# Four column blocks of x, the first weight split behind the turns, bias rows spread in DRAM, and fences given in two halves

## The chip, the cores and the metric

One core of one Trainium2 chip runs the whole program in one launch. The metric is device time in microseconds (us), the median of repeated executions; smaller is better.

## The reference

Two transformer layers are applied to 256 tokens of width 2048, all in float32. What matters here is the head of the first one and where its results go:

```python
h    = rms_norm(x, norm_mix)            # x: 256 x 2048
proj = h @ w_in                         # 2048 x 6168, cut into q, k, v, gates of three mixers
bias = rel_table[t5_bucket(distance)]   # one value per head and distance, 12 heads (layer 1), 8 heads (layer 2)
p    = exp(q @ k.T * scale + bias - max) ...
x    = x + mixed @ w_out;  x = x + cross_attention(...);  x = x + conv_ffn(...)     # layer 1
x    = x + (g_a * (nsa @ w_pa) + g_b * (deltanet @ w_pb)) @ w_o                     # layer 2
x    = x + square(relu(rms_norm(x) @ w_up)) @ w_down
```

Every dense product is one of 24 "gemms" over weights of about 500 MB in all. The two attentions with a relative bias add, for a query i and a key j, a value that depends on i - j and the head alone.

## The kernel before

**The gemms.** Weights lie in DRAM as items of 128 x 2048 float32 (1 MB; four k-tiles by 512 columns). SyncE issues one DMA for each item into one of four buffers `w_raw` (`Gemm.load`, L170); the load of item i+4 waits until VectorE has made the low part of item i. ScalarE rounds an item to `w_hi` (`make_hi`, L189), VectorE subtracts to get `w_lo` (`make_lo`, L194); both have two buffers, so the high part of item i+2 waits until TensorE is done with item i. TensorE multiplies each item three times (hi*hi, lo*hi, hi*lo; L282 to L284) for each of the two token tiles: 24 matmuls of 128x512. The left operand is `h_hi`/`h_lo`: x turned on TensorE against `ident` (L428, 32 transposes for 2048 columns), scaled by the gain and rounded on ScalarE (L441), its rest taken on VectorE (L455).

**Stages.** The program is a list of stages that TensorE, ScalarE and VectorE all walk through. After a stage each of them drains, signals, and waits for the two others (`stage_end`, L739), except where the stage is marked `unmet`: then nobody waits. Stage "start" loads nothing itself: its ScalarE part makes item 0's high part and waits for the gains and x, its VectorE part makes the low part, and all three meet. Stage "norm_mix" then turns x (`norm_to_lhs`, which calls `to_lhs`), makes item 1 on both engines and takes the root of the mean square of tile 0. Stage "win" is the first gemm: eight chunks of four items.

**The bias tables.** After the first chunk (items 0 to 3) TensorE multiplies the relative tables by a one-hot matrix (`toe_pe`, L810), VectorE adds (`toe_dve`, L816) and leaves two small tiles `tsum`: 12 and 8 partitions of 384 values. GpSimd's queue (`toe_pool`) writes each of these rows to DRAM 128 times over (`toe1`, `toe2`, laid out head, partition, value; L800), waits for both, and then goes on to the tables `tri`, `cmask` and the small weights. Much later `toeplitz` (L971) reads row p of a head's 128 copies with a start that moves by one value a partition, which gives the matrix over i - j.

**Together.** Five stages run a gemm and other work interleaved (`Together`). The work is cut into parts; after each gemm item q every engine does its share of parts (`done < (q+1) * parts // Q`), and ahead of them ScalarE and VectorE make the parts of item q+1. Between two works stands a fence (`pieces`): drain, add to the own `fenced` semaphore, wait for the two others. It stands at the head of the next work's first part. Where the next work's first part falls in the same item as the last part before it, nothing is between them; where it falls in the next item, the drain and the signal come after that item's `make_hi`/`make_lo` (or its 24 matmuls). The split of parts over items puts a gemm item between these works: small1 and turn1; small2 and turn2; turn2 and flat; unit2 and turn_qk; rates and delta0; state0 and delta1; gnorm and turn_ob (four items). After a stage's last work there is a fence too, and then the stage's own meeting.

Of the kernel before, what the change touches and what calls it, by code (L numbers as in the profile page):

```python
# [6 lines left out]
F32 = mybir.dt.float32  # L7
# [5 lines left out]
P = 128  # L13
S = 256
TT = S // P
D = 2048
KD = D // P
# [3 lines left out]
CH = 512  # L21
# [5 lines left out]
A_W, A_H, A_D = 768, 12, 64  # L27
# [11 lines left out]
N_H, N_G, N_D = 8, 2, 128  # L39
# [6 lines left out]
TOE = 384  # L46
# [25 lines left out]
def build(nc, t_in, out):  # L72

    ctx = ExitStack()
    with ctx:
# [3 lines left out]
        def sem(name):  # L79
            return ctx.enter_context(nc.semaphore(name))  # L80
# [16 lines left out]

        acc = [ctx.enter_context(nc.psum_tensor(f"acc{i}", [P, 512], F32)) for i in range(2)]
        wk = [ctx.enter_context(nc.psum_tensor(f"wk{i}", [P, 512], F32)) for i in range(6)]
        toe1 = nc.dram_tensor("toe1_scratch", (A_H, P, TOE), F32, kind="Internal").ap()  # L100
        toe2 = nc.dram_tensor("toe2_scratch", (N_H, P, TOE), F32, kind="Internal").ap()


        raw_ready = [sem(f"raw_ready{i}") for i in range(RAW)]
# [8 lines left out]
        stages = []  # L113


        class Gemm:
# [47 lines left out]
            def load(self, e):  # L164
                def body(n, first):
                    for j in range(self.ipc):
                        i = self.b + n * self.ipc + j
                        if not (first and self.b + j < RAW):
                            e.wait_ge(lo_ready, i - RAW + 1)
                        e.dma_start(w_raw[:, (self.slot(n, j)) % RAW, 0:self.cols(j)],  # L170
                                    self.w[bass.ds(n * self.ipc + j, 1), :, 0:self.cols(j)].rearrange(
                                        "a p f -> p (a f)")).then_inc(raw_ready[self.slot(n, j) % RAW], 16)
                self.chunks(e, body)
# [189 lines left out]
        class Together:  # L363
# [10 lines left out]

            def pieces(self, k, e):
                for i, w in enumerate(self.work):
                    yield from w.walk(k, e)

                    e.drain().then_inc(fenced[k], 1)
                    for other in fenced:  # L380
                        if other != k:
                            e.wait_ge(fenced[other], self.base + i + 1)

            def run(self, k, e):
                items = [(g, n, j) for g in self.gemms for n in range(g.n) for j in range(g.ipc)]
# [25 lines left out]
        turned_lo = sem("turned_lo")  # L411
        turns = [0]

        def to_lhs(src, n, hi, lo, kt0=0, gain=None):


            base = turns[0]
            turns[0] += n // 2
            W = len(wk)

            def pe(e):
                for p in range(n // 2):
                    if p >= W:
                        e.wait_ge(turned_lo, base + p - W + 1)
                    for i in (2 * p, 2 * p + 1):
                        for t in range(TT):
                            c = (i % 2) * S + t * P
                            mm = pe_.matmul(wk[p % W][:, c:c + P], src(t, i), ident[:], start=True, stop=True,  # L428
                                            is_transpose=True)
                    mm.then_inc(turned, 1)  # L430

            def act(e):
                for p in range(n // 2):
                    e.wait_ge(turned, base + p + 1)
                    b = wk[p % W]
                    if gain is None:
                        ins = act_.activation(hi[:, kt0 + 2 * p:kt0 + 2 * p + 2, :],
                                              b[:].rearrange("p (c s) -> p c s", c=2), ACT.Copy)
                    else:
                        for i in (2 * p, 2 * p + 1):  # L440
                            ins = act_.activation(hi[:, kt0 + i, :], b[:, (i % 2) * S:(i % 2 + 1) * S], ACT.Copy,  # L441
                                                  scale=gain[:, i:i + 1])
                    ins.then_inc(turned_hi, 1)

            def dve(e):
                for p in range(n // 2):
                    e.wait_ge(turned_hi, base + p + 1)
                    b = wk[p % W]
                    if gain is None:
                        k = slice(kt0 + 2 * p, kt0 + 2 * p + 2)  # L450
                        ins = dve_.tensor_tensor(lo[:, k, :], b[:].rearrange("p (c s) -> p c s", c=2),
                                                 hi[:, k, :].bitcast(F32), ALU.subtract)
                    else:
                        for i in (2 * p, 2 * p + 1):
                            ins = dve_.scalar_tensor_tensor(out=lo[:, kt0 + i, :], in0=b[:, (i % 2) * S:(i % 2 + 1) * S],  # L455
                                                            scalar=gain[:, i:i + 1], in1=hi[:, kt0 + i, :].bitcast(F32),
                                                            op0=ALU.mult, op1=ALU.subtract)
                    ins.then_inc(turned_lo, 1)
            return pe, act, dve
# [71 lines left out]
                e.wait_ge(squared, self.base + t + 1)  # L531
                return dve_.reciprocal(self.inv(t), st[:, 2 + t:3 + t])

        def norm_to_lhs(name, src, rows, hi, lo, gain, need=None):

            norm = Norm()
            norm.of(src, lambda t: rows[:, t, :])
            base = turns[0]  # L540
            tp, ta, td = to_lhs(lambda t, i: src[:, t, i * P:(i + 1) * P], KD, hi, lo, gain=gain)

            def pe(e):
                if need:
                    need(e)
                tp(e)

            def act(e):
                if need:
                    need(e)  # L550
                ta(e)
                norm.gemm.make_hi(e, 0, 1)
                norm.root(e, 0)

            def dve(e):
                td(e)
                norm.gemm.make_lo(e, 0, 1)
                norm.inverse(e, 0).then_inc(scaled, 1)
            s = Steps(name, pe, act, dve)
            s.unmet = True  # L560
            s.norm, s.lhs_from = norm, (base, 0)
            return s
# [194 lines left out]
        def got(e, name):  # L757
            if name not in landed:
                landed[name] = sem("in_" + name)
            e.wait_ge(landed[name], 16)  # L760
# [17 lines left out]

        rows0 = p1[:, :, 0:D]

        toe_mm, toe_row, toe_out, toe_dma = sem("toe_mm"), sem("toe_row"), sem("toe_out"), sem("toe_dma")
        tt1f = tt1[:].rearrange("p a b -> p (a b)")

        def toe_place(rows, slot, w):
# [6 lines left out]
        def toe_pool(e):  # L791
            for i in range(2):
                load(e, f"tw{i}", tw[i], t_in[f"onehot{i}"])
                load(e, f"trel{i}", trel[i], t_in[f"rel{i}"])
                load(e, f"tadd{i}", tadd[i], t_in[f"toe_add{i}"])
            e.wait_ge(toe_out, 2)


            for table, row, heads in ((toe1, tsum[0], A_H), (toe2, tsum[1], N_H)):
                e.dma_start(table, row.unsqueeze(1).to_broadcast([heads, P, TOE])).then_inc(toe_dma, 16)  # L800
            e.wait_ge(toe_dma, 32)
            load(e, "tri", tri[:], t_in["tri"])
            load(e, "cmask", cmask[:], t_in["cmask"])
        pool_steps.append(toe_pool)

        def toe_pe(e):
# [10 lines left out]

        def start_pe(e):
            got(e, "ident")
            got(e, "x")  # L820

        def start_dve(e):
            dve_.memset(ones[:], 1.0)
            dve_.memset(eps_c[:], EPS)
            Gemm.every[0].make_lo(e, 0, 0)
            got(e, "gains")

        def start_act(e):
            Gemm.every[0].make_hi(e, 0, 0)
            got(e, "gains")  # L830
            got(e, "x")
        stages.append(Steps("start", start_pe, start_act, start_dve))
        stages.append(norm_to_lhs("norm_mix", x, rows0, h_hi, h_lo, gains[:, 0, :]))
        mix = stages[-1]
        lhs = (h_hi, h_lo)

# [123 lines left out]
        def toeplitz(e, name, dst, table, heads, at_stage):  # L960

            landed[name] = sem("in_" + name)
            for k, sems in (at_stage.items() if isinstance(at_stage, dict) else ((k, at_stage) for k in at_end)):
                if isinstance(at_stage, dict):
                    e.wait_ge(fenced[k], sems)
                else:
                    e.wait_ge(at_end[k], sems)
            for h in range(heads):
                for c0, w, off in ((0, P, 255), (P, S, 127)):
                    src = bass.AP(tensor=table.tensor, offset=h * P * TOE + off, ap=[[TOE - 1, P], [1, w]])  # L970
                    e.dma_start(dst(h)[:, c0:c0 + w], src).then_inc(landed[name], 16)  # L971

        ab_hi = sem("ab_hi")
# [1080 lines left out]

        @block.sync
        def _(e):
            load(e, "x", x[:], t_in["x"])
            load(e, "gains", gains[:], t_in["gains"])
            load(e, "ident", ident[:], t_in["ident"])
            for g in Gemm.every:  # L2060
                g.load(e)

# [165 lines left out]
```

## Time and profile before

| | us |
|---|---|
| median of 3 runs | 3448.09 |
| lowest, highest | 3444.63, 3448.18 |
| profiled execution, its own time | 3446.6 |
| its span on the core | 3444.8 |
| TensorE (PE) busy | 3072.5 (89%) |
| VectorE (DVE) busy | 1596.7 (46%) |
| ScalarE (ACT) busy | 1312.6 (38%) |
| mean granted TensorE clock | 0.926 of full |
| DMA | 519.30 MB, mean 151 GB/s |

The page names engines PE (matmul), PEld (weight load), DVE, ACT, POOL (GpSimd) and SP (SyncE); a trailing q, as in DVEq, is an engine's sequencer (a drain or a semaphore). L194 is line 194 of the kernel. In a timeline the first two columns are the start and the duration in us, and the brackets give how long the engine was idle before and what ended it. In a table of windows each line is a stretch, its length, the busy time of each engine in it with the count of instructions, the granted TensorE clock, the busy share of the 16 DMA engines and the GB/s they moved.

### The profile page before, as it was taken

The page shows a single profiled execution, that of the slowest core. Times are in us where ns is not written, and L with a number is a line of the kernel's source. Part 1 is how long each engine was busy: PE and PEld are TensorE (multiplying, and loading weights), DVE is VectorE, ACT ScalarE, POOL GpSimd, SP SyncE. Part 2 cuts the span into 40 slices and gives each one's busy share as a digit, 9 for nine tenths or more (in the row PEclk, how much of TensorE's full clock was granted, in tenths as well). Part 3 has the DMA queues.
Part 4 walks back from the last instruction along what each step waited for, and adds up shares of the span by engine and source line. Part 5 has one row for each costly group of instructions (what it writes and reads, how often), then busy time and mean ns, then how long its engine had stood idle before and what let it go on. Part 6 is the DMA issues. An engine that isn't in the chain of part 4 may idle for free.

```text
span 3444.8 us, 36204 instructions
## 1 busy us (share of the span) xinstructions
PE 3072.5 (89%) x14022; PEld 2525.0 (73%) x14022; DVE 1596.7 (46%) x1648; ACT 1312.6 (38%) x1404; POOL 48.0 (1%) x89
## 2 busy tenths in 40 slices
PE   6798874998999999998997888799889999999997
PEld 5686554876887778776885676688768887888785
DVE  3332335455554445544424556444455544444443
ACT  3333231354443334434333334422233444334432
POOL 0001000000000000000001000000000000000000
PEclk9897775999999999999988999898999999999998
DMA  7643120543554455445525333222345555555553
GB/s 180 193 171 101 49 82 11 195 159 111 184 186 151 175 194 184 151 171 189 197 90 189 121 110 123 109 94 85 149 158 183 183 186 180 188 188 185 178 188 110
DMA packets 78180, 519.30 MB, mean 151 GB/s; under 512 B 10048, under 2 KB 10260, under 8 KB 24544
## 3 DMA queue, kind: packets, MB, share of 16 engines
q1 hardware_dynamic: 71280, 485.64, 39.2%
q0 software_dynamic: 6800, 32.28, 3.7%
q8 instruction: 68, 1.11, 0.1%
q14 instruction: 32, 0.26, 0.0%
HBM read 505.56 MB, written 12.32 MB: 150 GB/s over the span
## 4 chain that ended last, share of the span: by engine, by line
PE 82%; DVE 6%; ACT 4%; DMA 3%; issue 2%; DVEq 1%; ACTq 0%; another core or an unknown queue 0%; SPq 0%; POOL 0%; POOLq 0%; PEldq 0%
PE acc L282 24%; PE acc L284 23%; PE acc L283 23%; DMA w_raw<-in_w_win 2%; DVE w_lo L194 2%; PE wk L618 1%; ACT w_hi L189 1%; PE wk L649 1%; PE wk L1222 1%; PE wk L1128 1%; PE wk L1800 1%; PE wk L632 1%; ACT h_hi L441 1%; PE wk L1798 1%; PE wk L621 1%
## 5 line engine op out<-in xcount | busy, mean ns | idle before, releaser
L194 DVE TENSOR_TENSOR w_lo<-w_raw,w_hi 128x2048 fp32r<-128x2048 f32 (+2 forms) x492 | 1061.1, 2157 | 1257.9 <-ACT w_hi L189 1257.7
L189 ACT ACTIVATE w_hi<-w_raw 128x2048 fp32r<-128x2048 f32 (+2 forms) x492 | 889.2, 1808 | 1220.3 <-PE acc L284 1136.6
L282 PE MATMUL acc<-w_hi,h_hi 128*128 128x512 f32 x2656 | 1071.4, 403 | 102.1 <-DVE w_lo L194 45.7
L283 PE MATMUL acc<-w_lo,h_hi 128*128 128x512 f32 x2656 | 1055.1, 397 | 0.0
L284 PE MATMUL acc<-w_hi,h_lo 128*128 128x512 f32 x2656 | 1053.6, 397 | 0.0
L282 PEld LDWEIGHTS acc<-w_hi,h_hi 128*128 128x128 f32 x2656 | 515.1, 194 | 226.6 <-issue 64.2
L284 PEld LDWEIGHTS acc<-w_hi,h_lo 128*128 128x128 f32 x2656 | 513.9, 193 | 110.0
L283 PEld LDWEIGHTS acc<-w_lo,h_hi 128*128 128x128 f32 x2656 | 515.1, 194 | 104.0
L282 PE MATMUL acc<-w_hi,f_hi 128*128 128x512 f32 x856 | 341.5, 399 | 14.9 <-DVE x L330 7.0
L284 PE MATMUL acc<-w_hi,f_lo 128*128 128x512 f32 x856 | 339.6, 397 | 0.0
L283 PE MATMUL acc<-w_lo,f_hi 128*128 128x512 f32 x856 | 337.3, 394 | 0.0
L282 PEld LDWEIGHTS acc<-w_hi,f_hi 128*128 128x128 f32 x856 | 161.2, 188 | 57.5 <-DVE x L330 9.6
L284 PEld LDWEIGHTS acc<-w_hi,f_lo 128*128 128x128 f32 x856 | 161.2, 188 | 40.0
L283 PEld LDWEIGHTS acc<-w_lo,f_hi 128*128 128x128 f32 x856 | 161.3, 188 | 39.1
L282 PE MATMUL acc<-w_hi,oa_hi 128*128 128x256 f32 (+1 forms) x128 | 48.6, 379 | 39.0 <-DVE gm L2008 17.8
L1128 PE MATMUL wk<-tt 96*128 96x128 f32 x136 | 31.9, 430 | 40.0 <-DVE tt L1062 40.0
L1128 PEld LDWEIGHTS wk<-tt 96*128 96x128 f32 x136 | 29.6, 330 | 42.4 <-DVE tt L1062 31.8
L282 PEld LDWEIGHTS acc<-w_hi,oa_hi 128*128 128x128 f32 x128 | 26.5, 207 | 46.1 <-issue 19.4
L1819 ACT ACTIVATE wg<-wk 128x512 f32<-128x512 f32 x28 | 16.8, 599 | 112.9 <-PE wk L1791 112.9
L428 PE MATMUL wk<-ident,x 128*128 128x128 f32 x160 | 24.7, 324 | 35.2 <-DVEq L739 34.8
L428 PEld LDWEIGHTS wk<-ident,x 128*128 128x128 f32 x160 | 22.7, 170 | 37.7 <-issue 36.4
L441 ACT ACTIVATE h_hi<-wk,gains 128x256 fp32r<-128x256 f32 x96 | 36.7, 506 | 30.3 <-PE wk L428 30.2
(359 smaller groups left out, 2169.6 us busy)
## 6 DMA issues: line engine op xcount, KB each, us to landing
w_raw<-in_w_up_a SPq DMA_DIRECT2D x76, 1024.0 KB, 4.8
w_raw<-in_w_up_b SPq DMA_DIRECT2D x72, 1024.0 KB, 4.8
w_raw<-in_w_win SPq DMA_DIRECT2D x52, 1024.0 KB, 4.8
w_raw<-in_w_merge SPq DMA_DIRECT2D x32, 1024.0 KB, 4.8
w_raw<-in_w_down_a SPq DMA_DIRECT2D x32, 1024.0 KB, 4.8
w_raw<-in_w_down_b SPq DMA_DIRECT2D x32, 1024.0 KB, 4.8
w_raw<-in_w_win2g SPq DMA_DIRECT2D x24, 1024.0 KB, 4.8
w_raw<-in_w_down_a SPq DMA_DIRECT2D x24, 768.0 KB, 4.2
```

Of the source, the lines that this page charges most:

```text
L189: act_.activation(w_hi[:, s % SPL, 0:k], w_raw[:, s % RAW, 0:k], ACT.Copy).then_inc(hi_ready, 1)
L194: dve_.tensor_tensor(w_lo[:, s % SPL, 0:k], w_raw[:, s % RAW, 0:k], w_hi[:, s % SPL, 0:k].bitcast(F32), ALU.subtract).then_inc(lo_ready, 1)
L282: pe_.matmul(o, xh, wh, start=kt == 0, stop=False)
L283: pe_.matmul(o, xh, wl, start=False, stop=False)
L284: mm = pe_.matmul(o, xl, wh, start=False, stop=kt == K - 1)
L428: mm = pe_.matmul(wk[p % W][:, c:c + P], src(t, i), ident[:], start=True, stop=True, is_transpose=True)
L441: ins = act_.activation(hi[:, kt0 + i, :], b[:, (i % 2) * S:(i % 2 + 1) * S], ACT.Copy, scale=gain[:, i:i + 1])
L618: mm = pe_.matmul(o, u.q[:, qt * P:(qt + 1) * P], u.k[:, 0:len(kts) * u.kw], start=True, stop=not more)
L621: mm = pe_.matmul(o, a, b, start=False, stop=n == len(more) - 1)
L632: mm = pe_.matmul(tb[0:u.kw, c * P:(c + 1) * P], L[:, i % 2, at + n * u.kw:at + (n + 1) * u.kw], ident[:], start=True, stop=True, is_trans ...
L649: mm = pe_.matmul(ov[u.out % 2][p0:p1, qt * P:(qt + 1) * P], u.v(kt), PT[0:u.kw, i % 2, c * P:(c + 1) * P], start=u.first and n == 0 and q ...
L1128: mm = pe_.matmul(wk[2 * (l % 2) + t][:, h * P:(h + 1) * P], a[:, h, t * P:(t + 1) * P], b[:, h, t1 * P:(t1 + 1) * P], start=True, stop=True)
```

## The change

```diff
-        toe1 = nc.dram_tensor("toe1_scratch", (A_H, P, TOE), F32, kind="Internal").ap()
-        toe2 = nc.dram_tensor("toe2_scratch", (N_H, P, TOE), F32, kind="Internal").ap()
+        row1 = nc.dram_tensor("toe1_rows", (A_H, TOE), F32, kind="Internal").ap()
+        row2 = nc.dram_tensor("toe2_rows", (N_H, TOE), F32, kind="Internal").ap()
+        toe1 = nc.dram_tensor("toe1_scratch", (P, A_H * TOE), F32, kind="Internal").ap()
+        toe2 = nc.dram_tensor("toe2_scratch", (P, N_H * TOE), F32, kind="Internal").ap()
...
             def pieces(self, k, e):
                 for i, w in enumerate(self.work):
-                    yield from w.walk(k, e)
-
-                    e.drain().then_inc(fenced[k], 1)
                     for other in fenced:
-                        if other != k:
-                            e.wait_ge(fenced[other], self.base + i + 1)
+                        if i and other != k:
+                            e.wait_ge(fenced[other], self.base + i)
+                    parts = w.walk(k, e)
+                    for p in range(w.parts):
+                        next(parts)
+                        if p == w.parts - 1:
+                            for _ in parts:
+                                pass
+                            e.drain().then_inc(fenced[k], 1)
+                        yield
...
+                    if piece:                       # in to_lhs, TensorE's part, ahead of each pair of k-tiles
+                        piece(e, 2 * p * P)
...
                 ta(e)                               # in norm_to_lhs, ScalarE's part
+                if norm.gemm.b == 0:
+                    norm.gemm.make_hi(e, 0, 0)
                 norm.gemm.make_hi(e, 0, 1)
...
                 td(e)                               # in norm_to_lhs, VectorE's part
+                if norm.gemm.b == 0:
+                    norm.gemm.make_lo(e, 0, 0)
                 norm.gemm.make_lo(e, 0, 1)
...
-            for table, row, heads in ((toe1, tsum[0], A_H), (toe2, tsum[1], N_H)):
-                e.dma_start(table, row.unsqueeze(1).to_broadcast([heads, P, TOE])).then_inc(toe_dma, 16)
-            e.wait_ge(toe_dma, 32)
+            for rows, row in ((row1, tsum[0]), (row2, tsum[1])):
+                e.dma_start(rows, row).then_inc(toe_rows, 16)
             load(e, "tri", tri[:], t_in["tri"])
             load(e, "cmask", cmask[:], t_in["cmask"])
+            e.wait_ge(toe_rows, 32)
+            for table, rows, heads in ((toe1, row1, A_H), (toe2, row2, N_H)):
+                every = bass.AP(tensor=rows.tensor, offset=0, ap=[[0, P], [1, heads * TOE]])
+                e.dma_start(table, every).then_inc(toe_dma, 16)
+            e.wait_ge(toe_dma, 32)
...
         def start_pe(e):
             got(e, "ident")
-            got(e, "x")
...
-            Gemm.every[0].make_lo(e, 0, 0)          # start_dve
             got(e, "gains")
...
-            Gemm.every[0].make_hi(e, 0, 0)          # start_act
             got(e, "gains")
-            got(e, "x")
         stages.append(Steps("start", start_pe, start_act, start_dve))
-        stages.append(norm_to_lhs("norm_mix", x, rows0, h_hi, h_lo, gains[:, 0, :]))
+        stages[-1].unmet = True
+
+        def x_piece(e, c):
+            if c % CH == 0:
+                got(e, f"x{c // CH}")
+        stages.append(norm_to_lhs("norm_mix", x, rows0, h_hi, h_lo, gains[:, 0, :], piece=x_piece))
...
-                    src = bass.AP(tensor=table.tensor, offset=h * P * TOE + off, ap=[[TOE - 1, P], [1, w]])
+                    src = bass.AP(tensor=table.tensor, offset=h * TOE + off, ap=[[heads * TOE - 1, P], [1, w]])
...
-            load(e, "x", x[:], t_in["x"])
+            load(e, "ident", ident[:], t_in["ident"])
             load(e, "gains", gains[:], t_in["gains"])
-            load(e, "ident", ident[:], t_in["ident"])
+            for c in range(D // CH):
+                load(e, f"x{c}", x[:, :, c * CH:(c + 1) * CH], t_in["x"][:, :, c * CH:(c + 1) * CH])
```

The remarks behind # on changed functions are added here. In words: SyncE loads `ident` and the gains first and then x as four blocks of 512 columns (512 KB each); TensorE waits for a block only ahead of the turns that read it. Stage "start" no longer meets, and item 0 is split on ScalarE and VectorE after the turns. The bias rows go to DRAM once (30 KB in all), and two further DMAs, DRAM to DRAM, spread them to 128 copies of 18 KB and of 12 KB, partition outermost. `toeplitz` reads them with the new pitch. In `Together` an engine drains and signals right behind a work's last part, and waits for the others only ahead of the next work's first part; behind the last work it no longer waits.

## Rows read from the trace of the kernel before

**Rows 1.** The page: the chain that ended last, its lines.

```profile
PE acc L282 24%; PE acc L284 23%; PE acc L283 23%; DMA w_raw<-in_w_win 2%; DVE w_lo L194 2%; PE wk L618 1%; ACT w_hi L189 1%; PE wk L649 1%; PE wk L1222 1%; PE wk L1128 1%; PE wk L1800 1%; PE wk L632 1%; ACT h_hi L441 1%; PE wk L1798 1%; PE wk L621 1%
```

**Rows 2.** ScalarE in order of time, 0 to 45 us and 42 to 135 us.

```profile
12.49 1.91 ACT L189 ACTIVATE w_hi<-w_raw 128x2048 fp32r<-128x2048 f32 x1 [10.46 <-DMA w_raw<-in_w_win]
18.12 6.54 ACT L441 ACTIVATE h_hi<-wk,gains 128x256 fp32r<-128x256 f32 x16 [3.72 <-PE wk L428]
...
62.87 1.92 ACT L189 ACTIVATE w_hi<-w_raw 128x2048 fp32r<-128x2048 f32 x1 [3.52 <-PE acc L284]
94.25 1.91 ACT L189 ACTIVATE w_hi<-w_raw 128x2048 fp32r<-128x2048 f32 x1 [29.46 <-DMA w_raw<-in_w_win]
...
118.84 1.92 ACT L189 ACTIVATE w_hi<-w_raw 128x2048 fp32r<-128x2048 f32 x1 [2.95 <-PE acc L284]
124.28 1.92 ACT L189 ACTIVATE w_hi<-w_raw 128x2048 fp32r<-128x2048 f32 x1 [3.52 <-PE acc L284]
```

**Rows 3.** Windows of 5 us and less between 5 and 85 us.

```profile
5.00:10.00 5.00, 0.00 (x0) 0.00 (x0) 0.00 (x0) 0.00 (x0) 0.00 (x0) 1.00 1.00 357
10.00:15.00 5.00, 0.00 (x0) 0.00 (x0) 0.56 (x1) 1.91 (x1) 0.00 (x0) 1.00 1.01 419
...
45.00:50.00 5.00, 2.17 (x8) 0.59 (x6) 3.27 (x4) 1.91 (x1) 1.88 (x2) 1.00 0.02 3
50.00:53.00 3.00, 2.92 (x7) 2.34 (x8) 2.88 (x3) 0.00 (x0) 0.35 (x1) 0.53 1.00 85
53.00:56.00 3.00, 3.00 (x13) 2.42 (x13) 0.00 (x0) 0.00 (x0) 0.00 (x0) 0.90 0.96 76
```

**Rows 4.** DMA issues of the whole run: destination<-source, queue, count, KB each, us to landing.

```profile
w_raw<-in_w_win SPq DMA_DIRECT2D x52, 1024.0 KB, 4.8
gate_scratch<-x POOLq DMA_DIRECT2D x8, 512.0 KB, 3.6
toe_scratch<-tt POOLq DMA_DIRECT2D x1, 2304.0 KB, 41.2
result<-x POOLq DMA_DIRECT2D x1, 2048.0 KB, 6.6
toe_scratch<-tt POOLq DMA_DIRECT2D x1, 1536.0 KB, 72.7
tt<-in_norm_final POOLq DMA_DIRECT2D x1, 1024.0 KB, 6.2
```

**Rows 5.** TensorE in order of time, 0 to 45 us.

```profile
16.92 6.58 PE L428 MATMUL wk<-ident,x 128*128 128x128 f32 x32 [16.92 <-DVEq L739]
23.76 0.47 PE L282 MATMUL acc<-w_hi,h_hi 128*128 128x512 f32 x1 [0.26 <-issue]
```

**Rows 6.** TensorE, then VectorE, in order of time around four fences.

```profile
293.70 2.23 PE L485 MATMUL wk<-ident,p 128*128 128x128 f32 x16 [0.47 <-DVEq L379]
1785.32 1.06 PE L485 MATMUL wk<-ident,p 128*128 128x128 f32 x8 [1.51 <-DVEq L379]
2189.68 4.78 PE L485 MATMUL wk<-ident,pg 128*128 128x128 f32 x24 [11.18 <-DVEq L379]
...
1810.14 1.23 DVE L194 TENSOR_TENSOR w_lo<-w_raw,w_hi 128x1024 fp32r<-128x1024 f32 x1 [3.20 <-ACT w_hi L189]
1814.48 1.34 DVE L1509 MEMSET lp<- 128x1536 f32 x1 [3.11 <-PEq L379]
2187.21 2.28 DVE L194 TENSOR_TENSOR w_lo<-w_raw,w_hi 128x2048 fp32r<-128x2048 f32 x1
```

**Rows 7.** GpSimd in order of time, 0 to 250 us.

```profile
48.12 2.23 POOL L800 DMA_DIRECT2D toe_scratch<-tt  x2 [43.63 <-DVE tt L816]
```

**Rows 8.** VectorE in order of time, the start and 42 to 115 us.

```profile
14.44 2.29 DVE L194 TENSOR_TENSOR w_lo<-w_raw,w_hi 128x2048 fp32r<-128x2048 f32 x1 [13.41 <-ACT w_hi L189]
...
50.61 2.27 DVE L194 TENSOR_TENSOR w_lo<-w_raw,w_hi 128x2048 fp32r<-128x2048 f32 x1
```

**Rows 9.** TensorE behind the stage that holds flat.

```profile
1825.96 0.55 PE L282 MATMUL acc<-w_hi,oa_hi 128*128 128x256 f32 x1 [11.92 <-DVEq L739]
```

More of the change, by code:

```diff
@@ L412, in build, with to_lhs @@
         turns = [0]
-        def to_lhs(src, n, hi, lo, kt0=0, gain=None):
+        def to_lhs(src, n, hi, lo, kt0=0, gain=None, piece=None):
             base = turns[0]
@@ L532, in inverse, with norm_to_lhs @@
                 return dve_.reciprocal(self.inv(t), st[:, 2 + t:3 + t])
-        def norm_to_lhs(name, src, rows, hi, lo, gain, need=None):
+        def norm_to_lhs(name, src, rows, hi, lo, gain, need=None, piece=None):
             norm = Norm()
@@ L540, in norm_to_lhs @@
             base = turns[0]
-            tp, ta, td = to_lhs(lambda t, i: src[:, t, i * P:(i + 1) * P], KD, hi, lo, gain=gain)
+            tp, ta, td = to_lhs(lambda t, i: src[:, t, i * P:(i + 1) * P], KD, hi, lo, gain=gain, piece=piece)
             def pe(e):
@@ L779, in build @@
         rows0 = p1[:, :, 0:D]
-        toe_mm, toe_row, toe_out, toe_dma = sem("toe_mm"), sem("toe_row"), sem("toe_out"), sem("toe_dma")
+        toe_mm, toe_rows, toe_out, toe_dma = sem("toe_mm"), sem("toe_rows"), sem("toe_out"), sem("toe_dma")
         tt1f = tt1[:].rearrange("p a b -> p (a b)")
```

## The prediction

> **What bounds it now.** I read the page's chain first: TensorE's three products L282 to L284 are 70% of it, so the kernel is bound by TensorE, and the one foreign entry of size is `DMA w_raw<-in_w_win`, 2% [rows 1]. So a weight load of the first gemm is on the path, which in a stream prefetched four deep should not be. ScalarE in order of time shows where: it starts a new item every 5.44 us (118.84, 124.28), which is TensorE's 24 matmuls, but between 62.87 and 94.25 it stands, the last 29.46 us for that DMA [rows 2]. The windows tell what the DMA engines did: 1.00 and 0.96 busy while they moved only 85 and 76 GB/s, against 357 to 419 GB/s in the first 15 us [rows 3]. The issues name the culprit: the two writes of the bias rows, 2304 and 1536 KB, landed 41.2 and 72.7 us after issue, while a 1024 KB load usually takes 4.8 [rows 4]. Second, the very start: the first product stands at 23.76 [rows 5]. Third, waits at L379, the fences [rows 6].
>
> **Part 1: the bias rows.** Now: items between 62.87 and 118.84 are four, in 55.97 us; at 5.44 each they need 21.8. Lost: 34.2 us, low clock after the gaps included [rows 2]. The writes are issued from 48.12 on, and the later one lands at about 49.3 + 72.7 = 122 [rows 4, 7]. After: two writes of 30 KB together, then 2304 + 1536 KB = 3.93 MB from DRAM to DRAM. What made the old ones slow was not their volume: `result<-x`, 2048 KB from 128 partitions to DRAM, took 6.6 us, and `tt<-in_norm_final`, one row read from DRAM for 128 partitions, took 6.2 us for 1024 KB [rows 4]. Old source: 12 and 8 partitions; new source: one row repeated, in DRAM, which is the second case. No row shows DRAM to DRAM. Bounds for 3.93 MB: 3.75 x 3.3 = 12 us by the write of the result, 3.75 x 6.2 = 23 us by the repeated row, and from above the 74 us of now. I take 20 to 30 beside the weights, near the repeated row.
>
> What that does to the weights: load 9 is issued when low part 5 is done, 50.61 + 2.27 = 52.9 [rows 8], and unstalled its item would be wanted at 62.87 + 2 x 5.44 = 73.8: 20.9 us, of which a load uses 4.8, so 16 us of slack. The stream wants 1.05 MB per 5.44 us, 193 GB/s, of the 419 shown [rows 3]. If copy and weights share evenly, the weights get 210: no loss. If each copied byte costs the engines double (estimate), weights get a third, 140 GB/s, for 3.93 MB / 140 = 28 us: they fall behind by 28 x 53 / 1000 = 1.5 MB, 1.4 items, 7.7 us, less than 16. So the whole 34.2 us go. A copy as long as the 74 us of now would leave the stall as it is. `tri`, `cmask` and the small weights leave the queue 50 us earlier; the first stage that reads them follows the eight chunks of the first gemm, over 100 us on. The later reads by `toeplitz` keep count and size, the pitch alone changes; they have tens of us of cover, so nothing.
>
> The row shows a copy from repeated DRAM at 1024 KB in 6.2 us, 169 GB/s with its fixed time [rows 4]. The Trainium skill, "DMA: Bandwidth & Descriptors", section "Latency and other measured facts", gives some 207 to 214 GB/s per direction for copies between HBM tensors, about half of a load's rate; an estimate by that page is 3.93 MB / 210 = 19 us of all engines, between the bounds of 12 and 23. No run shows it yet.
>
> **Part 2: the start.** Now: item 0 lands and is split 12.49 to 16.73, and only behind the meeting, at 16.92, the turns start; the first product is at 23.76 [rows 2, 5, 8]. From first turn to ScalarE's last result are 18.12 + 6.54 - 16.92 = 7.7 us, set by ScalarE. After: SyncE issues ident, gains, x0; I take x0 as issued by 1.9. A 512 KB transfer with rows of 2 KB takes 3.6 us [rows 4]: x0 at about 5.5. The others follow at 357 GB/s, 1.5 us each, x3 at about 10; by its weight of turns (1.6 us of ScalarE a block) it isn't the limit. ScalarE ends the turns at 5.5 + 7.7 = 13.2, and item 0, behind the same bytes as now, is there at 12.5 to 13.5. Then high part to 15.2, low part to 17.5, first product 17.6: 6.2 us sooner. What was hidden before the turns (1.9 + 2.3) is now on the path; it is already in this sum. Item 1 (high 15.2 to 17.1, low 17.5 to 19.8) stays ahead of TensorE, as do the loads: load 4 is issued at 17.5 for 16.7 and wanted after 33.
>
> Against it: TensorE now stands from about 12.3 to 17.6. Between 45 and 50 it also stood for 2.8 of 5.0 us, and the next 3 us have a clock of 0.53, the 3 behind them 0.90 [rows 3]: 3 x 0.94 + 3 x 0.2 = 3.4 us at the lower of the two levels (1.2 GHz), which cost 1.7. I charge 1.7 (0 to 2). Net of the start: 4.5 us (2.5 to 6.5). The drop and rise in the row follow the rule of the Trainium skill, "TensorE: Matmul & The Clock Gate", section "Part 1: The HAM clock gate", that an idle TensorE falls to 1.2 GHz; by a rule that gaps are free the start would give 6.2.
>
> **Part 3: the fences.** Nothing is removed but the wait behind each last work; what moves is the signal, ahead of the next item's split. Only where a gemm item lies between two works does that matter (seven places).
> - small1 to turn1: TensorE stood 0.47. Gone: 0.5.
> - small2 to turn2: stood 1.51, since VectorE split an item before it signalled. TensorE's own item then ends it: 1.5.
> - turn2 to flat: VectorE stood 3.11 for TensorE's signal, which came behind 24 matmuls; behind flat TensorE stands 11.92 for VectorE [rows 9], so it shows in full. Next late is its own item split, done at 1810.14 + 1.23 = 1811.4, just where the 3.11 begin: 3.1.
> - unit2 to turn_qk: stood 11.18, of which the item split 2187.21 to 2189.49 goes: 2.2; VectorE's own long work stays.
> - rates to delta0, state0 to delta1, gnorm to turn_ob: TensorE stands 0.3 or less: 0.
> - five stage ends with one handshake less: 0.2 each (0 to 0.7), 1.0.
>
> [rows 6] Sum 8.3, I take 8.0 (5 to 11). A drain more or less costs nothing; their count is the same.
>
> **Sum.** 34.2 + 4.5 + 8.0 = 46.7. The profiled execution took 3446.6 (span 3444.8), so 3399.9; the median of the runs lies 1.5 above it: 3401.
>
> **Rivals.**
> - Coarse sharing: the copy's rows are 18 and 12 KB against 8 KB of a weight row. Each engine has 8 + 8 copy rows; if it alternates by rows, 16 weight rows, that is two items, pass among them. Over the 28 us of the double cost the stream wants 5.1 items, over 35 us (a slower copy) 6.4: 3.1 to 4.4 items or 17 to 24 us behind, less 16 of slack, with up to 2 of low clock behind the gap. I take 10 us that stay: 3411. For: nothing shows the sharing of these. Against: under the old writes, in far smaller rows, the weights were what starved.
> - The start gives nothing. In the trace x and the items behind it flow without a gap at 357 to 419 GB/s [rows 3], so four transfers should overlap. The Trainium skill, "DMA: Bandwidth & Descriptors", section "Bandwidth", says to batch to 1 MiB or more. Were a fixed time paid for each block, x3 would land at 1.9 + 4 x 3.6 = 16.3, the turns end 1.2 + 1.6 later at 19.1, and with 1.9 + 2.3 for item 0 the first product be at 23.4: 3405. The time from the block to the turns' end is taken from the rows of ScalarE [rows 2, 5].
> - The fences only hand the wait on, to a split that is late next: 3408. Against: the splits that would be late next end, in the rows, inside the time that the signal frees [rows 6].
> - It doesn't do what it says: the copy is as slow as the old writes, the stall stays: 3401 + 34 = 3435, still 0.4% faster.
> - The other side: DRAM to DRAM is read and written in the same memory; if it held the DMA engines twice as long as now, some 148 us, TensorE would stand 68 us instead of 34, from 48 on: 3435 + 34 = 3469. It is slower than before from the point where the stall exceeds 34.2 + 12.5 = 46.7 us. For: no row of such a copy. Against: the two fast rows above.
>
> **Chances.** Forecast 0.62, coarse sharing 0.17, start nothing 0.10, fences nothing 0.04, not what it says 0.04, other side 0.03. What a measurement can't tell from no change is 0.2%, 6.9 us. The first four are faster by more, and most of the fifth: faster 0.93, within 0.2% 0.04, slower 0.03. Range: from below 3389 (no clock loss, all seven fences and ends at their upper bound, runs scatter by 3), above 3418 (coarse sharing with its stall, start or fences short), which leaves out about 0.15.
>
> **What would show it.** In the trace after: the first product near 17.6 with a clock of half behind it for some 3 us; DMA issues with two copies landing in 20 to 30 us; ScalarE's item starts 5.44 us apart through 60 to 110 us, no wait on `w_raw<-in_w_win` above 2 us; idle at the four fences short by 0.5, 1.5, 3.1, 2.2. Wrong is the forecast if a wait of the 8th to 12th item for its DMA remains, or if the last x block lands after 12 us.

## The result, and the profile after

The changed kernel takes 3398.95 us (median of 4 runs, 3395.73 to 3405.03) against 3447.24 for the kernel before: 48.3 us less, a ratio of 0.9863 (95% interval 0.9846 to 0.988). Run again on another occasion it took 3399.97 against 3445.74, ratio 0.9864 (0.9849 to 0.9879). The forecast was 3401. The profiled execution took 3395.73, near the low end of its runs; its span went from 3444.8 to 3394.0.

The page's second line and chain of waits; the chain answers to [rows 1]. The load of the first gemm's weights has left it.

```profile
PE 3059.3 (90%) x14022; PEld 2515.1 (74%) x14022; DVE 1597.6 (47%) x1648; ACT 1313.1 (39%) x1404; POOL 47.8 (1%) x91
...
PE acc L284 24%; PE acc L286 24%; PE acc L285 24%; DVE w_lo L196 1%; PE wk L631 1%; PE wk L662 1%; ACT w_hi L191 1%; PE wk L1240 1%; PE wk L1146 1%; ACT h_hi L450 1%; PE wk L1818 1%; PE wk L645 1%; PE wk L1816 1%; PE wk L634 1%; PE wk L1809 1%
```

ScalarE of the changed kernel in order of time, against [rows 2]. From 56.76 on an item starts every 5.44 us, and all of them wait for TensorE, none for a load. The item that started at 118.84 before is the one at 83.96.

```profile
12.89 3.05 ACT L450 ACTIVATE h_hi<-wk,gains 128x256 fp32r<-128x256 f32 x8 [0.36 <-PE wk L437]
15.79 1.94 ACT L191 ACTIVATE w_hi<-w_raw 128x2048 fp32r<-128x2048 f32 x1
...
43.88 1.91 ACT L191 ACTIVATE w_hi<-w_raw 128x2048 fp32r<-128x2048 f32 x1 [1.98 <-PE acc L286]
56.76 1.92 ACT L191 ACTIVATE w_hi<-w_raw 128x2048 fp32r<-128x2048 f32 x1 [10.96 <-PE acc L286]
62.20 1.92 ACT L191 ACTIVATE w_hi<-w_raw 128x2048 fp32r<-128x2048 f32 x1 [3.52 <-PE acc L286]
...
83.96 1.92 ACT L191 ACTIVATE w_hi<-w_raw 128x2048 fp32r<-128x2048 f32 x1 [3.52 <-PE acc L286]
```

DMA issues of the changed kernel, against [rows 4]: the two copies take 14.8 and 21.0 us, where the writes out of on-chip memory took 41.2 and 72.7.

```profile
toe_scratch<-toe_rows POOLq DMA_DIRECT2D x1, 2304.0 KB, 14.8
x<-in_x SPq DMA_DIRECT2D x4, 512.0 KB, 8.0
toe_scratch<-toe_rows POOLq DMA_DIRECT2D x1, 1536.0 KB, 21.0
toe_rows<-tt POOLq DMA_DIRECT2D x1, 18.0 KB, 1.7
```

Windows of the changed kernel, against [rows 3]. Between 50 and 70 us the DMA engines are as busy as before, but move 344 to 376 GB/s; before, the same 5 us stretches had 78 to 148. TensorE is busy throughout. The two places where the clock falls are at 15 to 25 us and at 45 to 55 us.

```profile
0.00:5.00 5.00, 0.00 (x0) 0.00 (x0) 0.17 (x2) 1.28 (x1) 3.36 (x10) 1.00 0.42 110
5.00:10.00 5.00, 2.29 (x10) 1.89 (x11) 1.69 (x4) 1.68 (x4) 0.00 (x0) 1.00 0.97 300
...
18.00:21.00 3.00, 0.89 (x2) 0.79 (x3) 3.00 (x2) 3.00 (x2) 0.00 (x0) 0.50 0.85 360
21.00:25.00 4.00, 4.00 (x13) 3.14 (x13) 1.42 (x2) 2.35 (x4) 0.00 (x0) 0.68 0.96 348
...
50.00:55.00 5.00, 5.00 (x15) 3.95 (x14) 0.88 (x1) 0.00 (x0) 0.00 (x0) 0.57 1.00 362
55.00:60.00 5.00, 5.00 (x24) 4.12 (x23) 1.29 (x1) 1.92 (x1) 0.00 (x0) 1.00 1.00 344
60.00:65.00 5.00, 5.00 (x24) 4.14 (x23) 1.85 (x2) 1.92 (x1) 0.00 (x0) 1.00 0.97 376
```

TensorE of the changed kernel at the start, against [rows 5], and at the turns behind unit2, against [rows 6]. The first product is at 20.11 for 23.76; it waits 5.64 us for item 0's low part.

```profile
6.29 1.97 PE L437 MATMUL wk<-ident,x 128*128 128x128 f32 x8 [6.29 <-DMA x<-in_x]
9.68 4.79 PE L437 MATMUL wk<-ident,x 128*128 128x128 f32 x24 [1.42 <-DMA x<-in_x]
20.11 0.79 PE L284 MATMUL acc<-w_hi,h_hi 128*128 128x512 f32 x1 [5.64 <-DVE w_lo L196]
...
2136.88 4.35 PE L494 MATMUL wk<-ident,pg 128*128 128x128 f32 x24 [8.91 <-DVEq L388]
```

VectorE of the changed kernel around flat, against [rows 6]: the memset follows its item split after 0.27 us instead of 3.11.

```profile
1770.83 1.23 DVE L196 TENSOR_TENSOR w_lo<-w_raw,w_hi 128x1024 fp32r<-128x1024 f32 x1 [3.48 <-ACT w_hi L191]
1772.33 1.34 DVE L1527 MEMSET lp<- 128x1536 f32 x1 [0.27 <-issue]
...
1784.88 1.23 DVE L196 TENSOR_TENSOR w_lo<-w_raw,w_hi 128x1024 fp32r<-128x1024 f32 x1 [1.32 <-ACT w_hi L191]
```

One ruler serves below for all kernels, since runs differ by up to 10 us in later stages: the start of the twelfth low part (the fourth item of the third chunk) on VectorE. Behind it nothing of the stall or of the start is left open. Before: 120.78. Changed: 85.91, and 86.00 in its second profile. The ruler has a scatter of its own: five profiles of kernels that share the start and repeat the bias rows from DRAM (the two of the changed kernel, and old_shape, copy_twice and two_blocks below) put it between 83.85 and 86.00. Where a difference is under 2 us, the text therefore goes to the place itself.

### The profile page after: what moved, and what is told of

Same layout as the page of the kernel before. It is cut to its first block, busy times and chain, and to the rows that moved or that the text cites. A ratio compares the mean times of both kernels' runs of the same rounds, so it can differ in the third digit from the quotient of the medians.

```text
span 3394.0 us, 36191 instructions
## 1 busy us (share of the span) xinstructions
PE 3059.3 (90%) x14022; PEld 2515.1 (74%) x14022; DVE 1597.6 (47%) x1648; ACT 1313.1 (39%) x1404; POOL 47.8 (1%) x91
## 4 chain that ended last, share of the span: by engine, by line
PE 84%; DVE 6%; ACT 4%; DMA 2%; DVEq 1%; issue 1%; ACTq 0%; SPq 0%; POOL 0%; POOLq 0%; PEldq 0%
PE acc L284 24%; PE acc L286 24%; PE acc L285 24%; DVE w_lo L196 1%; PE wk L631 1%; PE wk L662 1%; ACT w_hi L191 1%; PE wk L1240 1%; PE wk L1146 1%; ACT h_hi L450 1%; PE wk L1818 1%; PE wk L645 1%; PE wk L1816 1%; PE wk L634 1%; PE wk L1809 1%
## 5 line engine op out<-in xcount | busy, mean ns | idle before, releaser
L693 ACT ACTIVATE l<-l,st 128x128 f32<-128x128 f32 (+1 forms) x40 | 17.9, 448 | 78.6 <-DVE st L725 78.6
L631 PE MATMUL wk<-tt 128*128 128x256 f32 (+3 forms) x160 | 46.9, 416 | 1.4 <-ACTq L752 0.7
```

The costliest lines, as they stand in the source:

```text
L631: mm = pe_.matmul(o, u.q[:, qt * P:(qt + 1) * P], u.k[:, 0:len(kts) * u.kw], start=True, stop=not more)
```

## The experiments

**The three parts, each alone on the kernel before.** The edits are the hunks of the diff above: for p1_rows the tables, `toe_pool` and `toeplitz`; for p2_start the loads, stage "start", `piece` and item 0 behind the turns; for p3_fences `pieces`.

> The kernel before with the bias rows alone changed (rows to DRAM once, spread DRAM to DRAM with the partition outermost, new pitch in toeplitz). Theory: the stall of the first gemm's weights was the two writes out of 12 and 8 partitions, and it is the whole of this part. Then 34 us less than before, about 3413, with ScalarE's item starts 5.44 us apart from the 7th item on, and the two copies landed some 15 and 21 us after issue. Rival A, part of the 34 us belongs to the earlier start (the loads run further ahead): then less than 30 us here. Rival B, later stages gain from the early tables as well: more than 40 us.

> The kernel before with the start alone changed (x in four blocks, item 0 split behind the turns, no meeting). The bias writes stay as they were. Theory: the first product comes 3.6 us sooner (20.1 for 23.8), some 2 us of that are left after the low clock that follows TensorE's idle 5.6 us, and the stall behind the old bias writes keeps its length, so 1 to 3 us less than before: about 3445. Rival A, the stall ends when the old writes end, and as these are issued by the same 2 us earlier nothing changes for it: same number. Rival B, the start gives the 4.5 us of the forecast: 3442 or less.

> The kernel before with the fences alone changed (drain and signal right behind a work's last part, wait ahead of the next work, none behind the last). Theory: each place gives what stood in its row, 0.5 + 1.5 + 3.1 + 2.2 us, and the stage ends some 1: 7 to 9 us less than before, about 3439. Rival, the further gain seen after the change (50.8 us of span in its profile for 34.9 at the 13th item) is the fences' too, through conv2 and the nsa stage: 14 us or more. If both are wrong and the waits are only handed on: 0 to 3.

| kernel | median us | ratio to before (95%) | 12th low part at |
|---|---|---|---|
| before | 3445.84 | | 120.78 |
| p1_rows | 3411.99 | 0.9901 (0.9886 to 0.9917) | 86.09 |
| p2_start | 3442.88 | 0.9994 (0.9985 to 1.0003) | 120.09 |
| p3_fences | 3438.92 | 0.9972 (0.996 to 0.9985) | 121.16 |

The rows take 33.9 us off, the fences 6.9, the start 3.0, which can't be told from nothing. The sum, 43.7, stands against 48.3 and 45.8 for all together; the intervals run from 28.6 to 39.3 us for the rows, from a loss of 1.0 to a gain of 5.2 for the start, and from 5.2 to 13.8 for the fences, so the parts add up as far as this can be seen. The rival that the early start fed the stall's end is out: p1_rows alone reaches the twelfth low part at 86.09, the changed kernel at 85.91. In p2_start the old writes are there again, and so is the stall:

```profile
toe_scratch<-tt POOLq DMA_DIRECT2D x1, 2304.0 KB, 41.0
toe_scratch<-tt POOLq DMA_DIRECT2D x1, 1536.0 KB, 72.9
```

For p3_fences the rival of 3 us or less falls. The rival of 14 or more lies just outside the interval, whose upper end is 13.8: the median speaks for 6.9, but two of the six runs are 13 and 17 us under the median of before, and the profiled one, with a span of 3431.4, is one of these. What the fences are worth in the whole run is known only as 5 to 14 us.

**What made the old writes slow: the source or the shape.** The changed kernel with the tables' old layout, the rows in DRAM still the source:

```diff
-                every = bass.AP(tensor=rows.tensor, offset=0, ap=[[0, P], [1, heads * TOE]])
+                every = bass.AP(tensor=rows.tensor, offset=0, ap=[[TOE, heads], [0, P], [1, TOE]])
```

> The changed kernel, but the spread tables keep the old layout: head outermost (12 and 8), then 128 copies, rows of 1.5 KB; the source is still the rows in DRAM, 3.93 MB in 2560 pieces. It tells which of two things made the old writes slow. Theory: the source, 12 and 8 partitions of on-chip memory that all the bytes came out of. Then the copies land in 15 to 35 us, the weights are not held, and the time is that of the changed kernel, 3399 within 4. Rival, the shape (an outermost dimension of 12 and 8, and pieces of 1.5 KB): then the copies take 40 us and more and 20 to 35 us of the stall are back, 3420 to 3435.

Measured 3397.15 us (3392.61 to 3403.36), ratio 0.9861 (0.9846 to 0.9876), twelfth low part at 83.85. The DMA issues of this kernel:

```profile
toe_scratch<-toe_rows POOLq DMA_DIRECT2D x1, 2304.0 KB, 19.8
toe_scratch<-toe_rows POOLq DMA_DIRECT2D x1, 1536.0 KB, 35.2
```

The shape costs something, 19.8 and 35.2 us for 14.8 and 21.0, but nothing on the path. With pieces and order of the destination as before, the change of source alone brings 41.2 down to 19.8 and 72.7 to 35.2, and the stall is gone. So the source, rows on 12 and 8 partitions of on-chip memory that were read 128 times each, was the cause. Whether it was the small number of partitions, the repeated reading of the same on-chip bytes, or on-chip memory as such, the runs don't separate: no kernel here repeats rows from more partitions. The one row that bears on it is `result<-x`, 2048 KB out of 128 partitions and read once, in 6.6 us.

**How far the copies are from hurting.** The changed kernel with the pair of copies issued a second time when the first has landed:

```diff
             e.wait_ge(toe_dma, 32)
+            for table, rows, heads in ((toe1, row1, A_H), (toe2, row2, N_H)):
+                every = bass.AP(tensor=rows.tensor, offset=0, ap=[[0, P], [1, heads * TOE]])
+                e.dma_start(table, every).then_inc(toe_dma, 16)
+            e.wait_ge(toe_dma, 64)
```

> The changed kernel with the two DRAM to DRAM copies made twice, one pair behind the other (the queue waits for the first pair): twice the suspected cost. Theory: the copy is wholly hidden, because copy and weights share the DMA engines at 315 to 376 GB/s and the weights have 16 us of slack, used only while a copy runs; the second pair, some 21 us more, uses that slack anew or a little further, so the time stays at 3400 within 3 and ScalarE's item starts stay 5.44 us apart up to the 20th. Rival (coarse sharing, from the forecast), the weights lose ground under the copy all the time and the single copy only just ends before the slack does: then the second pair brings a wait of the 12th to 15th item for its load, of 5 to 20 us: 3405 to 3420.

Measured 3398.2 us (3396.58 to 3402.43), ratio 0.9865 (0.985 to 0.9881). Its windows, over both pairs (48 to 91 us):

```profile
50.00:60.00 10.00, 10.00 (x44) 8.22 (x43) 2.64 (x2) 1.92 (x1) 0.00 (x0) 0.95 1.03 375
60.00:70.00 10.00, 10.00 (x46) 8.28 (x45) 4.58 (x2) 4.52 (x3) 0.00 (x0) 1.00 0.97 365
70.00:80.00 10.00, 10.00 (x46) 8.29 (x45) 4.46 (x3) 3.83 (x2) 1.03 (x2) 1.00 1.02 356
80.00:90.00 10.00, 10.00 (x45) 8.29 (x45) 3.70 (x3) 3.83 (x2) 0.00 (x0) 1.00 0.96 358
```

The DMA engines are full, and TensorE never stands. The copy moves 3.93 MB in about 21 us, 187 GB/s; from the first pair's issue to the second's are 22.4 us, from there to the queue's next instruction 20.8. No item waits for its load, so coarse sharing with its 10 us that stay is refuted. But the copy isn't free for the weights. Of some 359 GB/s over these 43 us the two pairs take 183, which leaves at most 176 for a stream that wants 193, and its loads land late. This is from issue to landing, least, median and most, of the weight loads issued between 48 and 91 us:

```profile
DMA to landing us min/median/max: 9.5/12.5/16.5
```

Without a copy it is 4.8. The longest, load 9, was issued at 50.5 and landed at 67.0, 4.2 us ahead of its item. Under the second pair the load issued at 75.7 landed after 14.4 us, at 90.1, and its item started at 93.0: only 2.9 us were left. Then the loads caught up, before the second pair had ended (12.4 and 9.9 us). So the sharing lies near the even one of the forecast's first case, but it costs the weights a part of their rate. It is hidden because the loads are issued far enough ahead.

**Is it TensorE's idleness that lowers the clock at the start?** 20 matmuls of the identity by itself between the turns and the first product, into a bank that nothing reads (the trace shows two records for each):

```diff
                 tp(e)
+                if norm.gemm.b == 0:
+                    for _ in range(20):
+                        pe_.matmul(acc[1][:, 0:P], ident[:], ident[:], start=True, stop=True)
```

> The changed kernel once more, on the chip of the next three, which are compared with it. Expected 3399, within its earlier runs of 3396 to 3405.

> The changed kernel with 20 idle matmuls (identity by identity, 128x128, into a bank that nothing reads) on TensorE between the last turn of x and the first product, some 4.6 us at 0.23 us each. Theory: TensorE's 5.6 us of idleness there is what puts the first product at the lower clock (0.50 and 0.68 in the windows 18 to 25 us), which costs 2.3 us. Then the first item runs at 5.44 us, the third item's low part starts some 2 us sooner than 29.5, the first product itself stays at 20.1, and 2 us less in all: 3397. Rival, the low clock does not hang on that gap, or the filler delays the first product: no change, 3399 or more.

The changed kernel: 3399.97 (3397.74 to 3402.47), as expected. With the filler: 3394.56 (3390.62 to 3398.2), ratio 0.9847 (0.9834 to 0.9861). Windows of filler:

```profile
15.00:18.00 3.00, 3.00 (x26) 3.00 (x25) 2.08 (x5) 3.00 (x4) 0.00 (x0) 1.00 1.00 423
18.00:21.00 3.00, 2.76 (x21) 2.46 (x20) 3.00 (x2) 3.00 (x2) 0.00 (x0) 1.00 0.72 306
21.00:25.00 4.00, 4.00 (x19) 3.29 (x18) 1.21 (x2) 1.79 (x4) 0.00 (x0) 1.00 0.93 340
```

The first product stands where it stood (20.04), but the clock stays at 1.00 where it was 0.50 and 0.68. The third item's low part starts at 27.79 for 29.52 and 30.88, the twelfth at 82.87 for 85.91 and 86.00: 3.0 us gained at that point. So it is the gap that lowers the clock, to 1.2 GHz by its level.

What it costs is read at the place, from the first product to the third low part. That takes 7.75 us with the filler. It takes 9.41 in the changed kernel and 10.57 in its second profile, and in the other profiles with a gap of 5.1 to 5.6 us there 9.44 (two_blocks), 9.47 (old_shape), 9.92 (copy_twice), 9.97 (toe_early) and 10.56 (p2_start). The gap costs 1.7 to 2.8 us, then. The rest of the 3.0 against the first profile isn't the filler's: from the fourth low part to the seventh, across the second gap, that profile took 23.75 us, the second one 22.49 and filler 22.44.

**The second gap.** TensorE's two products of the tables ahead of item 3 instead of behind it:

```diff
                     for j in range(self.ipc):
+                        if first and j == 3 and "pe" in self.after_first:
+                            self.after_first["pe"](e)
                         self.pe_item(e, n, j, first)
-                    if first and "pe" in self.after_first:
-                        self.after_first["pe"](e)
```

> The changed kernel with TensorE's two small products of the bias tables ahead of item 3 instead of behind it. Theory: behind item 3 VectorE waits for them before it makes item 4's low part, so TensorE stands 2.9 us and then runs at a clock of 0.57 for 5 us; ahead of item 3 the additions fall into VectorE's idle time. Then no window between 40 and 60 us is below a clock of 1.00, item 6's low part starts 5 us sooner than 58.7, and the time is 5 less: 3394. Rival, the gap only moves ahead of item 3 (VectorE's addition stands before the low part of item 4 all the same) and the time stays at 3399.

Measured 3393.59 us (3391.14 to 3398.03), ratio 0.9848 (0.9835 to 0.9862), twelfth low part at 80.72: 5.2 us gained. From its fourth low part to the seventh are 17.89 us, for 23.75 and 22.49 in the two profiles of the changed kernel, so the second gap with its low clock costs 4.6 to 5.9. Windows of toe_early, in which TensorE doesn't stand and the clock doesn't fall:

```profile
40.00:45.00 5.00, 5.00 (x22) 3.86 (x21) 3.21 (x3) 1.67 (x2) 3.18 (x6) 1.00 0.74 263
45.00:50.00 5.00, 5.00 (x23) 4.13 (x22) 2.61 (x2) 1.92 (x1) 0.00 (x0) 1.00 1.00 364
50.00:55.00 5.00, 5.00 (x23) 4.13 (x22) 1.91 (x2) 1.92 (x1) 0.00 (x0) 1.00 1.04 317
```

**The size of the blocks.** Two blocks of 1024 columns instead of four of 512, in the loads and in `x_piece`:

```diff
-            for c in range(D // CH):
+            for c in range(D // (2 * CH)):
```

> The changed kernel with x in two blocks of 1024 columns (rows of 4 KB) instead of four of 512 (2 KB). The forecast put the last block at 10 us and the first product at 17.6; the trace has 11.7 or later and 20.1. Theory: rows of 2 KB move more slowly. Then the last block is there 1 to 2 us sooner, the first one later (about 8), and the first product at 19 to 20, for less than 1 us in all: 3398 to 3399. Rival, the number of transfers or the later issue costs, not the row: the first product comes 1 to 2 us sooner or later by that alone. With one block in all, the other end, it would be near 9.6 + 2 + 7.

Measured 3397.48 us (3392.85 to 3401.36), ratio 0.9862 (0.9847 to 0.9877). TensorE of two_blocks at the start:

```profile
8.06 6.23 PE L437 MATMUL wk<-ident,x 128*128 128x128 f32 x32 [8.06 <-DMA x<-in_x]
19.93 0.80 PE L284 MATMUL acc<-w_hi,h_hi 128*128 128x512 f32 x1 [5.64 <-DVE w_lo L196]
```

Its window from 5 to 10 us has 375 GB/s for the 300 of four blocks:

```profile
5.00:10.00 5.00, 1.94 (x9) 1.94 (x10) 0.00 (x0) 0.79 (x2) 0.00 (x0) 1.00 1.03 375
```

So x as a whole moves faster, as the theory has it (the last block landed at about 10.9 us for 13.0), the first block comes 1.8 us later, the turns then run without a break, and the first product is at 19.93 for 20.11: gain and loss cancel. Whether it is the longer rows or the smaller number of transfers that moves faster, this doesn't tell.

**Both gaps closed.**

> The changed kernel with both edits that came out faster: the products of the bias tables ahead of item 3, and 20 idle matmuls between the turns and the first product. Each alone took about 6 us off (3394 for 3400). Theory: they touch two different gaps, at 15 to 20 and at 45 to 50 us, and add up: 3388 to 3390. Rival: what each gained was in part a later stretch that happened to run at the higher clock in these runs; then the sum stays at 3392 to 3394.

Measured 3392.07 us (3385.12 to 3394.46), ratio 0.984 (0.9827 to 0.9854), the lowest of all kernels here and 53.6 us under before. The twelfth low part starts at 77.29: 8.6 us before the changed kernel's, and 3.0 + 5.2 = 8.2 had come of the two alone. Place by place the 8.6 are 1.2 of a first product that stood at 18.94 instead of 20.11, which neither edit was meant to move, 1.6 at the first gap (7.83 us for 9.41) and 5.9 at the second (17.89 for 23.75). So at the places of the edits each gives what it gave alone; that the two totals lie so close is in part luck. The medians, 3400.0, 3394.6, 3393.6 and 3392.1, show less than a sum; with runs that spread over 7 to 9 us they can't decide it.

## Why the prediction was right

**The stall** went as worked out: 34.2 us forecast. Over the same four items the old trace took 118.84 - 62.87 = 55.97 us, the new one 83.96 - 62.20 = 21.76. Alone on the kernel before it was worth 33.9. The copy was given 20 to 30 us and took 14.8 and 21.0 beside the weights, which makes the repeated row (6.2 us for 1024 KB in [rows 4], 23 us for the whole) the right row to size by. The Trainium skill ("DMA: Bandwidth & Descriptors", section "Latency and other measured facts") gives 207 to 214 GB/s per direction for copies between HBM tensors where the row pitch doesn't slow them. The trace is a tenth under that, in another setting: 3.93 MB in some 21 us, beside a stream of weights, is 187 GB/s. No run has the copy alone.

The slack was worked out for load 9, as 16 us, but load 8 has less: it was issued at 50.2 and its item was wanted at 62.87 + 5.44 = 68.3, which is 18.1, less 4.8 for the load 13.3 us. The conclusion stands on that too. But the case of even sharing, "no loss", was too kind: in the changed kernel load 8 landed after 11.3 us and load 9 after 16.3, 5.8 us ahead of its item.

**The start** is the term that was mis-sized: 4.5 us forecast (2.5 to 6.5). At the twelfth low part the changed kernel is 0.2 us ahead of p1_rows, p2_start 0.7 ahead of before; old_shape, two_blocks and copy_twice, which share the start, are 1.9 to 2.2 ahead of p1_rows. So it is worth 0.2 to 2.2 us there, and 3.0 in the median, with an interval that holds zero, and 4.5 as well; what speaks against 4.5 is the place, not the median. Two steps of its working were off, the landing times by much and the clock by little.
- The landing times. x0 was put at 5.5 and came at 6.29; the last block was put at about 10; the third landed only at 11.7, by the chain of waits, and the last at about 13.0, with 300 GB/s in the window 5 to 10 us where I had taken the 357 of [rows 3]. A last block that lands after 12 us was one of the two signs by which the forecast said that it would be wrong. That sign came, and it marks this part: the start, not the stall. The 3.6 us taken for a block were those of a write out of on-chip memory; the load of the first block took 4.6. ScalarE's turns thus ended at 15.9, not 13.2, with waits of 1.7 and 0.4 us among them, and the first product came at 20.1, not 17.6. two_blocks, with 375 GB/s in that window, shows that the cut into four costs rate. In the first 5 us 110 GB/s were moved, where the kernel before moved 210: there x was issued at 0.76 us, here its first block at 1.68, behind ident and the gains, and the weights behind four issues of 0.65 us each. How much that order costs was not tried.
- The clock. The gap of 5.64 us costs 1.7 us in the profile of the changed kernel, as charged, and up to 2.8 in others; 0 to 2 had been allowed. In that profile the second gap took more as well: from the item at 43.88 to the next are 12.88 us, where they were 11.55. That isn't an effect of the change: its second profile has 11.61, and p3_fences, which has the old start, 12.38.

**The fences** were put at 8.0 and are 6.9 in the median. Place by place the trace gives what stood in the rows: at turn_qk TensorE stands 8.91 for 11.18, so 2.3; from the item split ahead of flat to the first of the next stage are 14.05 us for 16.85, so 2.8; the 1.51 and 0.47 at the other two are gone from the waits of TensorE, which keep two for this line, 8.9 and 0.3:

```profile
PE wk L494 <- DVEq L388: 9.2, 2, 8.9
```

That is 7.1 for the 7.3 of the four places, and nothing was late next. For the stage ends (1.0) no row was found, so no run shows that term. The interval of p3_fences, 5.2 to 13.8, holds the 8.0.

**What is left over**: 48.3 measured and 46.7 forecast. It is not to be explained, and that the total came so close, with a start that gave less than forecast, is luck within the scatter of the runs. The two profiles of the changed kernel are 6.1 us apart, though they agree to 0.1 us at the twelfth low part and within 1.9 us up to 1820 us; they part between 1820 and 2130 us, where the granted clock was 0.91 and 0.96 in the one and 0.88 and 0.93 in the other. A difference of a few us between two kernels says nothing unless it shows at the place of the edit.

**The rivals.** Coarse sharing is refuted by copy_twice, since no item waits, though with 2.9 us to spare at the least; and the other side and "not what it says" by p1_rows. "The start gives nothing" was nearly right in the number, by another way than the one described: the blocks did overlap, but came late, and the clock took much of the rest. "The fences give nothing" is refuted by p3_fences.

## What to carry to other kernels

A DMA that keeps the engines busy at a fraction of their rate holds up every other transfer; look at busy share and GB/s side by side, and then at its source: here it was rows on 12 and 8 partitions of on-chip memory, each read 128 times. Write a small tile to DRAM once and repeat it from there, and judge the copy by a row that also repeats its source. Then compare the landing times of the other loads with their slack: that no engine waited doesn't say how near it was. When work is moved from ahead of TensorE's first use to behind it, count the gap that opens, and the low clock behind it, as part of the price; idle matmuls in the gap, or the small products moved ahead of the last item, take it back.

## What the runs showed of the hardware that was not expected

The DMA engines shared themselves between a DRAM to DRAM copy with rows of 12 to 18 KB and loads with rows of 8 KB so that the loads, which asked for 193 GB/s, were not late once in 43 us at 356 to 375 GB/s in all, though those issued meanwhile took 9.5 to 16.5 us to land instead of 4.8. A gap on TensorE of 2.9 to 5.6 us was followed by some 3 to 6 us of products at the lower clock, and 20 matmuls whose result nobody reads kept it at the higher one.
